# Upper half of the first output panel one copy earlier, and sample numerators of the mLSTM on two column tiles

## The chip, the cores and the metric

The kernel runs on one core of a Trainium2 chip. A core has five engines that run their own instruction streams and meet at semaphores: PE (TensorE, matrix products into PSUM), DVE (VectorE), ACT (ScalarE), POOL (GpSimd) and SP (SyncE, which here only issues DMAs). The metric is the device time of the core in microseconds, from one execution of the whole program; lower is better.

## The reference

Two layers of a decoder trunk run for a prompt of 512 tokens and for 8 sample sequences of 8 tokens each (64 tokens). Each layer is a half-step SwiGLU FFN, a mixer, a second half-step FFN and a gated embedding; layer 0 mixes with latent attention, layer 1 with an mLSTM. All inputs are float32. Cut to what the change touches:

```python
def swiglu(h, w_in, w_out):
    a, b = jnp.split(h @ w_in, 2, axis=-1)
    return (jax.nn.silu(a) * b) @ w_out
...
# one chunk of the mLSTM, per batch b and head h (t, s: tokens; d: 128 keys; v: 256 values)
S = jnp.einsum('bhtd,bhsd->bhts', qc, kc) * jnp.exp(logD - m_t[..., None])
num = jnp.einsum('bhts,bhsv->bhtv', S, vc) + decay[..., None] * jnp.einsum('bhtd,bhdv->bhtv', qc, C)
den = jnp.sum(S, axis=-1) + decay * jnp.einsum('bhtd,bhd->bht', qc, n)
```

For the sample group each of the 8 sequences has its own state C (128 x 256 for a head), so the 64 sample tokens of a head are multiplied by eight different matrices, eight tokens each.

## The kernel before

Activations are kept transposed, channels on partitions and the 576 tokens (512 + 64) on the free axis. A float32 product is made of three products of split operands: a value is an upper part, rounded by a copy to the matmul's format, and a lower part, the rest. For a weight panel in `raw`, ACT writes the upper part `whi` (`upper`, line 1790) and POOL or DVE the lower part `wlo` (`lower`, line 1736, and `panel_lower`, line 2212). A panel is 128 columns of a weight matrix, eight or six chunks of 128 rows.

**The FFNs.** There are four, two in each layer. The 22 hidden blocks of an FFN are cut into three parts of 6, 8 and 8 blocks (`PARTS`), twelve parts in all. In a part PE first makes the hidden blocks one after the other (`pair`, `block_product`, lines 2523 to 2525): seven products of 12 matmuls each, counted by the semaphore `w_done`. Between them ACT copies partial sums from one PSUM bank to another (`copied`, line 1833): the first copy after product 1, the second after product 2, the third after product 3 and the fourth after product 5. PE waits for them by `w_copied`. ACT then applies the SiLU (`gate`), DVE multiplies (`gated`), ACT splits the result (`u_upper`) and DVE its lower part. After the last block of a part PE multiplies the part's hidden values by eight output panels of `w_out` (`out_tile`, which calls `products`, lines 2461 to 2466), one tile of 128 output channels each. A tile may start only when both halves of its panel are there; its chunk n waits for hidden block n.

Every engine runs its instructions in the order in which they stand. The order on ACT is written out in `ffn` (line 1846): a block at a time, with the splitting of the next block's weights between the copies. For the last block of a part (`not more`) there is no next block, and the upper half of the part's first output panel is made instead. It stands behind the fourth copy and ahead of the block's `gate`. It waits for the panel's data (`raw_ready`), for the earlier panels' products and for product 4 of the block before, which is the last to read that slot of `whi`. POOL makes the lower half of the first two panels, DVE of the other six. SP loads the first two panels as soon as their slots of `raw` are free, which is a block before the part's end.

**The mLSTM.** Heads are run one after the other, four in all. For a head PE makes the numerators of the four prompt tiles (`numerators`, line 1563), an output gate panel and the next head's stabilisers, then the sample numerators (`sample_numerators`, lines 1566 to 1576), the states of the samples and of the prompt (`states`, line 1582, `prompt_state`, line 1589) and the next head's scores. `sample_numerators` accumulates nine products of 257 columns in one PSUM bank (256 values and the normaliser), 64 rows high: the within-chunk product, and one for each sequence. The stationary operand of sequence b is a slice of `qdm` that holds the queries of the eight tokens of b in their own columns and zeros in the other 56, so each product writes 64 rows and adds zeros to 56 of them. DVE copies the result to `nu` (line 1404), updates the denominators (lines 1430 to 1439) and then the states `Cb` (line 1409), for which PE waits in turn. ACT makes the next head's decays meanwhile (`decays`, lines 1223 to 1231).

Of the kernel before, what the change touches and what calls it, by code (L numbers as in the profile page):

```python
# [19 lines left out]
TP, TS = 512, 64  # L20
# [3 lines left out]
NB, TB = 8, 8  # L24
# [6 lines left out]
LH, DK, DV = 4, 128, 256  # L31
# [37 lines left out]
def pairs_before(p):  # L69

    n = 0
    for f, name in enumerate(FFNS):
        for q, (a, b) in enumerate(PARTS):
            if p >= P0[name + "_out"] + 8 * q:
                n = NC_F * f + b
    return n
# [62 lines left out]
def hybrid_step(nc, ins, outs):  # L139
    I = ins  # L140
    with ExitStack() as ctx:
        def sem(name):
            return ctx.enter_context(nc.semaphore(name))
# [73 lines left out]
        ps = nc.psum_tensor("ps", [P, 8, 512], F32)  # L217
        ps = ctx.enter_context(ps)
# [28 lines left out]
        w_done, w_copied, w_act = sem("block_products"), sem("sums_copied"), sem("gate_input")  # L247
# [9 lines left out]
        def flat_g(t, i):  # L257

            return t[:, i % 2, :, :].rearrange("p (q c) m -> p q (c m)", q=2)
# [810 lines left out]
        Vt = lu.put("Vt", [P, NTT, LH, DV + 1])  # L1070
        kt = lu.put("kt", [P, NTT, LH, DK])
        Cb = lu.put("Cb", [P, NB, DV + 1])
# [12 lines left out]
        qdm = lu.put("qdm", [P, NB * QDW])  # L1085
# [5 lines left out]
        SD = (SDa, SDb)  # L1091
# [22 lines left out]
        B1, B2, B3, B4, B5 = B0 + 1, 4, 5, 6, 7  # L1114
# [366 lines left out]
        def mlstm_pes(pe, v, products, sums, token_sums, spread, tiles, xgh, xgl):  # L1481
            mm, tr = nc.tensor.matmul, nc.tensor.transpose
# [84 lines left out]
            def sample_numerators(h):  # L1567

                pe.wait_ge(l_SD, NTT * (h + 1))
                pe.wait_ge(l_in, h + 1)  # L1570
                pe.wait_ge(l_nu, 5 * h + 3)
                out = ps[0:TS, B5, 0:DV + 1]
                mm(out, SD[h % 2][0:TS, 1280:1280 + TS], Vt[0:TS, 4, h, :], start=True, stop=False)
                for b in range(NB):
                    ins = mm(out, qdm[:, b * TS:(b + 1) * TS], Cb[:, b, :], start=False, stop=b == NB - 1)
                ins.then_inc(l_num, 1)

            def states(h, b):
# [202 lines left out]
        def _(act):  # L1781
# [8 lines left out]
            def upper(p, dyn, n, place=None, back=1):  # L1790
                hi = place[0] if place else whi[:, p % SPLIT, :, :]
                act.wait_ge(raw_ready[p % RAW], UNIT * (p // RAW - 1 + pairs_before(p) // 2) + dyn * (UNIT // RAW))
                act.wait_ge(panel_used, p - back + dyn)
                act.activation(hi[:, 0:n, :], raw[:, p % RAW, 0:n, :], ACT.Copy).then_inc(whi_ready, 1)  # L1794
# [25 lines left out]
            def third_upper(part, i):  # L1820
                act.wait_ge(g_sum, part.blocks(i, 3))
                act.activation(flat_g(g3h, i), flat_g(g3f, i), ACT.Copy).then_inc(g_hi, 1)  # L1822

            def fourth_upper(part, i):
                g, h = part.g0 + i, 2 * part.half(i) + 1
                act.wait_ge(raw_ready[h], part.loaded(i, h))
                if g:
                    act.wait_ge(w_done, 7 * g)
                act.activation(blocks(g4h), raw_pair(part, i)[:, 3, :], ACT.Copy).then_inc(g_hi, 1)

            def copied(part, i, n, after, dst, src):
                act.wait_ge(w_done, 7 * (part.g0 + i) + after)
                act.activation(dst, src, ACT.Copy).then_inc(w_copied, 1)  # L1833
# [5 lines left out]
            def gate(part, i):  # L1839
                g = part.g0 + i  # L1840
                act.wait_ge(w_act, 2 * g + 2)
                if g:
                    act.wait_ge(w_ub, g)
                act.activation(sA[:, :], tA[:, :], ACT.Silu).then_inc(silu_done, 1)  # L1844

            def ffn(f, last_upper, nxt):
                for part in PART[f]:
                    for i in range(part.n):
                        g, more = part.g0 + i, i + 1 < part.n
                        A, C, B, D_ = [ps[:, part.bank(i) + k, 0:HT] for k in range(4)]  # L1850
                        embed = not part.k and not i
                        if i:
                            fourth_upper(part, i)
                        copied(part, i, 1, 1, B, A)
                        if i == 1 and part.q == 0:
                            gate(part, 0)
                        if i:
                            u_upper(part, i - 1)
                        if g:
                            act.wait_ge(w_act, 2 * g - 1)  # L1860
                        copied(part, i, 2, 2, p5[:, :], D_)
                        if embed:
                            embed_square(0)
                            embed_square(1)
                        if more:
                            first_upper(part, i + 1)
                        copied(part, i, 3, 3, C, B)
                        if embed:
                            embed_square(2)
                            embed_square(3)  # L1870
                        if more:
                            second_upper(part, i + 1)
                        if more:
                            third_upper(part, i + 1)
                        copied(part, i, 4, 5, D_, B)
                        if embed:
                            embed_square(4)
                        if i == 0 and part.q == 0:
                            r_copy(FFNS[f], 1)
                        if not more:  # L1880
                            act.wait_ge(w_done, 7 * (g - 1) + 4)
                            upper(part.p, 0, part.n)
                        if i or part.q:
                            gate(part, i)
                    u_upper(part, part.n - 1)
                    upper(part.p + 1, 0, part.n)
                    if part.q < 2:
                        after = PART[f][part.q + 1]
                        for k in range(2, 8):
                            upper(part.p + k, 0, part.n)  # L1890
                        second_upper(after, 0)
                        third_upper(after, 0)
                        first_upper(after, 0)
                        fourth_upper(after, 0)
                    else:
                        for k in range(8):
                            if k < 6:
                                upper(part.p + 2 + k, 0, part.n)
                            elif k == 6:
                                upper(part.p + 8, 0, last_upper)  # L1900
                            act.wait_ge(tile_taken, part.t + k + 1)
                            x_scaled_upper(nxt, k)
                            x_squares(nxt, k)
# [843 lines left out]
```

## Time and profile before

| | us |
|---|---|
| median of three runs | 2567.34 |
| lowest and highest | 2565.26, 2567.75 |
| the profiled execution, its whole time | 2565.75 |
| its span, first to last instruction | 2563.8 |
| PE busy | 2473.5 (96%) |
| DVE busy | 1684.0 (66%) |
| ACT busy | 1073.0 (42%) |
| POOL busy | 307.7 (12%) |

The granted clock of TensorE is 0.989 of full in the mean. The profiled execution took 1.95 us more than its span and lies 1.59 us under the median. PE is busy in 96% of the span, so most of what other engines do is hidden behind it; what counts is where PE waits, and how long its own instructions take. Line numbers in the profile are those of the kernel before. In the changed kernel lines behind 1575 stand four lower down the file, so a line 1794 of before is 1798 there.

### The profile page before, as it was taken

Reading aid. Unit: us, or ns where it says so; the run is one execution under the profiler, and the core shown is the slowest. Engines: PE = TensorE matmul, PEld = TensorE weight load, DVE = VectorE, ACT = ScalarE, POOL = GpSimd, SP = SyncE. Lnnn points to the kernel's source line nnn. Section 1 sums busy time; section 2 is a strip of 40 time slices with the busy share of each in tenths; the row PEclk is TensorE's granted clock in tenths of the full one; section 3 lists DMA queues with packets and bytes.
Section 4 is the critical chain, followed back from the end, with each engine's and each line's share of the span. In section 5 each row is a group of like instructions: output and inputs, shape, how many; then the busy total and the mean of one; then the engine's idle time right before and its main releaser. Section 6 shows DMA issues by size and latency. Waiting matters only on the chain.

```text
span 2563.8 us, 45161 instructions
## 1 busy us (share of the span) xinstructions
PE 2473.5 (96%) x17653; PEld 2355.3 (92%) x17653; DVE 1684.0 (66%) x2398; ACT 1073.0 (42%) x1780; POOL 307.7 (12%) x247
## 2 busy tenths in 40 slices
PE   6999999999899999999998999999999999999998
PEld 5999999877688999999998999999997789999998
DVE  6676675888555586848568585765434586857666
ACT  6444353455333453525445353443133354443532
POOL 0000001202330100000030000001322200000012
PEclk9999999999899999999999999999999999999999
DMA  4233232222232222333222333332323222332322
GB/s 121 83 99 91 83 94 78 52 49 75 72 110 77 58 79 87 99 87 94 84 78 78 91 91 91 90 91 71 92 69 103 87 66 82 99 99 82 96 76 72
DMA packets 410806, 216.44 MB, mean 84 GB/s; under 512 B 40085, under 2 KB 407834, under 8 KB 410650
## 3 DMA queue, kind: packets, MB, share of 16 engines
q1 hardware_dynamic: 404646, 209.17, 29.0%
q10 hardware_dynamic: 2420, 3.37, 0.4%
q0 software_dynamic: 3584, 1.84, 0.4%
q8 instruction: 95, 1.56, 0.2%
q14 instruction: 61, 0.50, 0.1%
HBM read 206.57 MB, written 7.76 MB: 84 GB/s over the span
## 4 chain that ended last, share of the span: by engine, by line
PE 87%; DVE 7%; ACT 3%; issue 2%; POOL 1%; DMA 0%; SPq 0%; ACTq 0%; DVEq 0%; POOLq 0%
PE ps L2461 13%; PE ps L2463 13%; PE ps L2466 13%; PE ps L2523 12%; PE ps L2524 12%; PE ps L2525 12%; PE ps L1010 2%; DVE st L628 1%; PE ps L924 1%; POOL wlo L1739 1%; PE ps L886 1%; PE ps L875 1%; PE ps L1563 1%; PE ps L972 1%; PE ps L994 1%
## 5 line engine op out<-in xcount | busy, mean ns | idle before, releaser
L1739 POOL TENSOR_TENSOR wlo<-raw,whi 128x1024 fp32r<-128x1024 f32 (+2 forms) x96 | 207.6, 2163 | 1823.0 <-ACT whi L1794 1823.0
L1794 ACT ACTIVATE whi<-raw 128x1024 fp32r<-128x1024 f32 (+2 forms) x175 | 169.4, 968 | 433.1 <-PE ps L2466 432.1
L2461 PE MATMUL ps<-uh,whi 128*128 128x320 f32 (+1 forms) x1408 | 302.2, 296 | 8.0 <-POOL wlo L1739 7.3
L2463 PE MATMUL ps<-ul,whi 128*128 128x320 f32 (+1 forms) x1408 | 301.1, 295 | 0.0
L2466 PE MATMUL ps<-uh,wlo 128*128 128x320 f32 (+1 forms) x1408 | 301.1, 295 | 0.0
L2461 PEld LDWEIGHTS ps<-uh,whi 128*128 128x128 f32 x1408 | 215.9, 188 | 10.7 <-issue 10.5
L2228 DVE TENSOR_TENSOR ub<-ps,r 128x576 f32<-128x576 f32 x96 | 72.7, 757 | 230.7 <-PE ps L2466 215.0
L2466 PEld LDWEIGHTS ps<-uh,wlo 128*128 128x128 f32 x1408 | 216.0, 188 | 0.0
L2463 PEld LDWEIGHTS ps<-ul,whi 128*128 128x128 f32 x1408 | 216.0, 188 | 0.0
L2147 DVE TENSOR_TENSOR wlo<-raw,whi 128x1024 fp32r<-128x1024 f32 x88 | 107.8, 1225 | 130.3 <-ACT whi L1814 130.3
L2461 PE MATMUL ps<-xh,whi 128*128 128x320 f32 x752 | 164.2, 300 | 3.3 <-DVE RB L1280 2.7
L2463 PE MATMUL ps<-xl,whi 128*128 128x320 f32 x752 | 160.6, 295 | 0.0
L2466 PE MATMUL ps<-xh,wlo 128*128 128x320 f32 x752 | 160.4, 295 | 0.0
L1844 ACT ACTIVATE sA<-tA 128x576 f32<-128x576 f32 x88 | 60.4, 686 | 238.5 <-DVE tA L2184 238.5
L1833 ACT ACTIVATE ps<-ps 128x288 f32<-128x288 f32 x264 | 104.3, 395 | 108.3 <-PE ps L2525 107.6
L1822 ACT ACTIVATE g3h<-g3f 128x1024 fp32r<-128x1024 f32 x88 | 93.5, 1062 | 92.1 <-DVE g3f L2141 87.9
L2181 DVE TENSOR_TENSOR ps<-ps,p 128x576 f32<-128x576 f32 x88 | 66.9, 760 | 85.5 <-PE ps L2525 74.0
L2461 PEld LDWEIGHTS ps<-xh,whi 128*128 128x128 f32 x752 | 115.9, 189 | 4.6 <-DVE RB L1280 2.9
L2523 PE MATMUL ps<-xAh,whi 128*128 128x288 f32 x352 | 106.6, 303 | 12.0 <-issue 12.0
L2463 PEld LDWEIGHTS ps<-xl,whi 128*128 128x128 f32 x752 | 115.9, 189 | 0.0
L2466 PEld LDWEIGHTS ps<-xh,wlo 128*128 128x128 f32 x752 | 115.7, 189 | 0.0
L2523 PE MATMUL ps<-xTh,g3h 128*128 128x288 f32 x352 | 104.3, 296 | 5.2 <-DVE xTl L2290 3.7
(425 smaller groups left out, 7085.3 us busy)
## 6 DMA issues: line engine op xcount, KB each, us to landing
raw<-in_w_ffa_in SPq DMA_DIRECT2D x88, 512.0 KB
raw<-in_w_ffb_in SPq DMA_DIRECT2D x88, 512.0 KB
raw<-in_w_ffa_out SPq DMA_DIRECT2D x32, 512.0 KB
pages<-in_cache_ckv SPq DMA_DIRECT2D x128, 128.0 KB, 2.0
raw<-in_w_ffb_out SPq DMA_DIRECT2D x32, 512.0 KB
raw<-in_w_mlstm_in SPq DMA_DIRECT2D x24, 512.0 KB
raw<-in_w_ple_gate SPq DMA_DIRECT2D x16, 512.0 KB
raw<-in_w_ffa_out SPq DMA_DIRECT2D x16, 384.0 KB
```

Of the source, the lines that this page charges most:

```text
L1739: pool.tensor_tensor(lo[:, 0:n, :], raw[:, p % RAW, 0:n, :], hi[:, 0:n, :].bitcast(F32), ALU.subtract).then_inc(wlo_ready, 1)
L1794: act.activation(hi[:, 0:n, :], raw[:, p % RAW, 0:n, :], ACT.Copy).then_inc(whi_ready, 1)
L1822: act.activation(flat_g(g3h, i), flat_g(g3f, i), ACT.Copy).then_inc(g_hi, 1)
L1833: act.activation(dst, src, ACT.Copy).then_inc(w_copied, 1)
L2147: dve.tensor_tensor(wlo[:, s, :, :], raw[:, 2 * part.half(i), :, :], whi[:, s, :, :].bitcast(F32), ALU.subtract).then_inc(g_lo, 1)
L2228: dve.tensor_tensor(ub[:, :], slot(part.t + c, bank), r[:, :], ALU.mult).then_inc(out_read, 1)
L2461: mm(out[:, t], hi[:, n, :], xh_n[:, t], start=first and n == 0, stop=False)
L2463: mm(out[:, t], hi[:, n, :], xl_n[:, t], start=False, stop=False)
L2466: ins = mm(out[:, t], lo[:, n, :], xh_n[:, t], start=False, stop=end)
L2523: mm(out, w_h, m_h, start=fresh and n == 0, stop=False, skip_group_check=not fresh)
L2524: mm(out, w_h, m_l, start=False, stop=False, skip_group_check=not fresh)
L2525: ins = mm(out, w_l, m_h, start=False, stop=n == 3, skip_group_check=not fresh)
```

## The change

Two edits, independent of each other.

1. In ACT's order for the last block of a part, the upper half of the part's first output panel moves from behind the fourth copy to between the third and the fourth, with the wait that belongs to it. That holds for all twelve parts.
2. `sample_numerators` writes its 64 rows as two column tiles of 32. Sequences 0 to 3 own rows 0 to 31, sequences 4 to 7 rows 32 to 63. The within-chunk product is made twice, once for each half, and the eight sequence products take 32 columns of `qdm` in place of 64 and alternate between the halves (0, 4, 1, 5, ...). That makes ten products in place of nine, each with half the rows.

```diff
-                out = ps[0:TS, B5, 0:DV + 1]
-                mm(out, SD[h % 2][0:TS, 1280:1280 + TS], Vt[0:TS, 4, h, :], start=True, stop=False)
-                for b in range(NB):
-                    ins = mm(out, qdm[:, b * TS:(b + 1) * TS], Cb[:, b, :], start=False, stop=b == NB - 1)
+                half = TS // 2
+                for o in (0, half):
+                    mm(ps[o:o + half, B5, 0:DV + 1], SD[h % 2][0:TS, 1280 + o:1280 + o + half], Vt[0:TS, 4, h, :],
+                       start=True, stop=False)
+                for k in range(NB // 2):
+                    for b, o in ((k, 0), (k + NB // 2, half)):
+                        ins = mm(ps[o:o + half, B5, 0:DV + 1], qdm[:, b * TS + o:b * TS + o + half], Cb[:, b, :],
+                                 start=False, stop=k == NB // 2 - 1)
                 ins.then_inc(l_num, 1)
...
                         if more:
                             third_upper(part, i + 1)
+                        if not more:
+                            act.wait_ge(w_done, 7 * (g - 1) + 4)
+                            upper(part.p, 0, part.n)
                         copied(part, i, 4, 5, D_, B)
                         if embed:
                             embed_square(4)
                         if i == 0 and part.q == 0:
                             r_copy(FFNS[f], 1)
-                        if not more:
-                            act.wait_ge(w_done, 7 * (g - 1) + 4)
-                            upper(part.p, 0, part.n)
```

ACT's instructions at the end of the first part (six blocks), before: the fourth block copy is the second of the two that stand in one row, and `whi<-raw` with 128x768 is the output panel.

```order
L1833 ACTIVATE ps<-ps 128x288
L1837 ACTIVATE uh_67<-ub_88 128x576
L1833 ACTIVATE p5_90<-ps 128x288
L1833 ACTIVATE ps<-ps 128x288 x2
L1794 ACTIVATE whi_51<-raw_50 128x768
L1844 ACTIVATE sA_87<-tA_86 128x576
L1837 ACTIVATE uh_67<-ub_88 128x576
```

And in the changed kernel, at the same place:

```order
L1837 ACTIVATE ps<-ps 128x288
L1841 ACTIVATE uh_67<-ub_88 128x576
L1837 ACTIVATE p5_90<-ps 128x288
L1837 ACTIVATE ps<-ps 128x288
L1798 ACTIVATE whi_51<-raw_50 128x768
L1837 ACTIVATE ps<-ps 128x288
L1848 ACTIVATE sA_87<-tA_86 128x576
L1841 ACTIVATE uh_67<-ub_88 128x576
```

One instruction moved past one copy. PE's instructions around the sample numerators of head 0, before:

```order
L1534 MATMUL ps<-RE,cf 128x72
L1573 MATMUL ps<-Vt,SDa 64x257
L1575 MATMUL ps<-Cb,qdm 64x257 x8
L1582 MATMUL ps<-Vt,kwb 128x257 x4
L1589 MATMUL ps<-Vt,kw 128x257 x4
```

And in the changed kernel:

```order
L1534 MATMUL ps<-RE,cf 128x72
L1574 MATMUL ps<-Vt,SDa 32x257 x2
L1578 MATMUL ps<-Cb,qdm 32x257 x8
L1586 MATMUL ps<-Vt,kwb 128x257 x4
L1593 MATMUL ps<-Vt,kw 128x257 x4
```

Nothing moved there; the rows in the result of each product are halved and one product is added.

## Rows read from the trace of the kernel before

**Rows 1.** The page: busy time by engine, and the chain that ended last.

```profile
PE 2473.5 (96%) x17653; PEld 2355.3 (92%) x17653; DVE 1684.0 (66%) x2398; ACT 1073.0 (42%) x1780; POOL 307.7 (12%) x247
...
PE 87%; DVE 7%; ACT 3%; issue 2%; POOL 1%; DMA 0%; SPq 0%; ACTq 0%; DVEq 0%; POOLq 0%
```

**Rows 2.** Groups by form: busy, mean ns of one | idle before, its releasers.

```profile
L2461 PE MATMUL ps<-uh,whi 128*128 128x320 f32 x704 | 218.4, 310 | 8.0 <-POOL wlo L1739 7.3 <-issue 0.7
```

**Rows 3.** Timeline (start, us, what), end of an 8-block part: ACT, POOL, DVE.

```profile
375.38 0.40 ACT L1833 ACTIVATE ps<-ps 128x288 f32<-128x288 f32 x1 [1.12 <-PE ps L2525]
...
378.58 0.40 ACT L1833 ACTIVATE ps<-ps 128x288 f32<-128x288 f32 x1 [2.81 <-PE ps L2525]
378.89 1.05 ACT L1794 ACTIVATE whi<-raw 128x1024 fp32r<-128x1024 f32 x1
...
380.02 2.39 POOL L1739 TENSOR_TENSOR wlo<-raw,whi 128x1024 fp32r<-128x1024 f32 x1 [134.83 <-ACT whi L1794]
...
384.00 0.76 DVE L2173 TENSOR_TENSOR ul<-ub,uh 128x576 fp32r<-128x576 f32 x1 [0.75 <-ACT uh L1837]
...
384.99 2.40 POOL L1739 TENSOR_TENSOR wlo<-raw,whi 128x1024 fp32r<-128x1024 f32 x1 [2.58 <-ACT whi L1794]
```

**Rows 4.** Timeline of PE: an earlier part's last panel (149.27), then this part's end.

```profile
149.27 0.43 PE L2466 MATMUL ps<-uh,wlo 128*128 128x320 f32 x2
149.53 0.30 PE L2523 MATMUL ps<-xAh,whi 128*128 128x288 f32 x1
...
381.45 0.29 PE L2525 MATMUL ps<-xTh,g4l 128*128 128x288 f32 x1
382.67 0.50 PE L2461 MATMUL ps<-uh,whi 128*128 128x320 f32 x2 [0.92 <-POOL wlo L1739]
...
389.13 0.44 PE L2461 MATMUL ps<-uh,whi 128*128 128x320 f32 x2
```

**Rows 5.** Bandwidth in 40 slices from 362 to 376 us (0.35 us each).

```profile
GB/s 0 0 0 51 203 252 329 348 348 347 304 291 288 217 18 0 0 0 0 0 0 0 0 0 0 0 0 0 0 0 0 0 0 0 32 108 197 350 348 347
```

**Rows 6.** Timeline, end of a 6-block part: PE and POOL.

```profile
108.89 1.85 POOL L1739 TENSOR_TENSOR wlo<-raw,whi 128x768 fp32r<-128x768 f32 x1 [57.55 <-ACT whi L1794]
...
110.54 0.29 PE L2525 MATMUL ps<-xTh,g4l 128*128 128x288 f32 x1
...
111.00 0.50 PE L2461 MATMUL ps<-uh,whi 128*128 128x320 f32 x2 [0.16 <-issue]
...
113.87 1.85 POOL L1739 TENSOR_TENSOR wlo<-raw,whi 128x768 fp32r<-128x768 f32 x1 [3.13 <-ACT whi L1794]
...
115.87 0.50 PE L2461 MATMUL ps<-uh,whi 128*128 128x320 f32 x2
```

**Rows 7.** Timeline of PE, sample numerators of head 0.

```profile
1919.29 0.65 PE L1573 MATMUL ps<-Vt,SDa 64*64 64x257 f32 x2
1919.87 3.69 PE L1575 MATMUL ps<-Cb,qdm 128*64 128x257 f32 x16
1923.49 1.56 PE L1582 MATMUL ps<-Vt,kwb 64*128 64x257 f32 x6
```

**Rows 8.** Instructions of line 1575 (all heads): count, ns min/median/max, starts; form.

```profile
L1575 PE MATMUL ps<-Cb,qdm x64: 377/379/432, 1919.9 to 2019.3; 128*64 128x257 f32 x64
```

**Rows 9.** Line 886 from 560 to 570 us: its forms, then its timeline.

```profile
L886 PE MATMUL ps<-PT,Vp x16: 272/433/644, 563.8 to 565.9; 128*64 128x512 f32 x4, 128*64 128x384 f32 x4, 128*64 128x256 f32 x4, 128*64 128x128 f32 x4
...
563.77 2.38 PE L886 MATMUL ps<-PT,Vp 128*64 128x512 f32 x16
```

**Rows 10.** Timeline of ACT and DVE around the sample numerators of head 0.

```profile
1922.32 0.64 ACT L1229 ACTIVATE SDb<-Md,cols 128x128 f32<-128x128 f32 x2
...
1923.60 0.42 DVE L1404 COPY nu<-ps 64x257 f32<-64x257 f32 x1 [3.38 <-PE ps L1575]
...
1925.86 0.16 DVE L1437 TENSOR_TENSOR den<-den 128x5 f32<-128x5 f32 x1
```

**Rows 11.** Stretch from 2002 to 2036 us: busy PE, PEld, DVE, ACT, POOL, then PEclk, DMA.

```profile
2002.00:2036.00 34.00, 29.55 (x163) 23.98 (x162) 15.15 (x44) 8.88 (x18) 9.13 (x6) 0.95 0.38 119
```

## The prediction

> **What bounds the kernel now.** I read the page first: PE is busy in 96% of the span and makes 87% of the chain that ended last [rows 1]. So a gain comes from two places only, a wait of PE that goes or PE work that gets shorter. Then the groups of instructions by form, for what ends PE's idle time ahead of each line: ahead of the products of `uh`, that is of the output tiles, PE waits 7.3 us for POOL's lower half `wlo` [rows 2]. In the timeline this is one wait of 0.92 us at the end of each 8-block part (rows 4 show one; there are eight such parts, and the eight waits read alike), and 8 x 0.92 = 7.36 accounts for the 7.3.
>
> **Edit 1, what it removes.** The chain at the end of an 8-block part: PE ends product 5, ACT makes the fourth copy at 378.58 and then the upper half from 378.89, POOL the lower half from 380.02 to 382.41 [rows 3]; PE starts the tile at 382.67, 0.26 later, while its own last product was issued at 381.45 [rows 4]. ACT stood idle for 2.81 us ahead of the fourth copy [rows 3]. Behind the third copy (375.38) the upper half starts at 375.38 + 0.31 = 375.69 (0.31 is the step from the fourth copy's start to the upper's in the same rows), ends at 376.74, and POOL, 1.13 behind ACT's start as now, runs from 376.82 to 379.21. With 0.26 the tile could start at 379.5, and PE comes for it at 381.58. So the wait goes, with 2.1 us to spare.
>
> What does it do to the fourth copy, which now queues behind the upper? ACT is free at 376.74 and the copy isn't due before 378.58: nothing, with 1.8 us to spare. Does the panel's data stand ready at 375.7? It is the only DMA wait that is moved, and an in-order ACT would hold the fourth copy and so PE. The transfers of the part's first two panels run from about 363 to 367 us [rows 5], so 8 us are to spare. No DMA issue moves. POOL has nothing else there (134.83 us idle ahead of it), so its queue delays nobody.
>
> What is late next? A seam at which nothing waits is the one from a part's last panel to the next part's first block: the pair of matmuls from 149.27 is followed at 149.53 without a gap [rows 4]. So the tile starts 0.13 behind 381.45, at 381.58 in place of 382.67: 1.09 us. After a stall the first weight load also lies open, which makes the first pair 0.50 long in place of 0.43 or 0.44 [rows 4]: another 0.06. That is 1.15 for an 8-block part. The last chunk needs the hidden block's lower half, ready at 384.76 [rows 3], while the tile has 8 chunks in 389.13 - 382.67 = 6.46 us and comes to its last one some 5.5 us after its start, at 387.1. The second tile would start at 381.58 + 6.46 - 0.06 = 387.98; its lower half is ready at 384.99 + 2.40 = 387.39 [rows 3], with 0.26 on top 387.65. That is still ahead, by 0.3 us only, so I keep it as a rival. Later panels are released by PE's progress and move with it. Eight parts: **8 x 1.15 = 9.2 us**. The lower bound is the bare waits, 7.4.
>
> The four 6-block parts are different. There the tile starts at 111.00, 0.26 behind POOL's end at 110.74, and 0.46 behind the last product's start [rows 6]. The page calls it issue, yet it is the same wait, and 0.33 us would go. But the second tile starts at 115.87, while the second panel's lower half is ready only at 113.87 + 1.85 = 115.72 [rows 6]. That one hangs on the last block's `gate` and `u_upper`, which the edit doesn't advance. PE would come for it at 115.5 and wait. I count **0** for these four; the upper bound is 4 x 0.33 = 1.3.
>
> **Edit 2, what it removes.** Each float32 product shows as two records, two passes of PE. The eight sequence products are 16 passes in 3.69 us [rows 7]; with the last one's 0.38 [rows 8] taken off, 15 steps in 3.31, or 0.22 a pass. From line 1573 to line 1582 it is 1923.49 - 1919.29 = 4.20 us for 18 passes [rows 7], 3.96 of it passes and the rest the two changes of shape.
>
> Afterwards there are 20 passes, ten on each tile. What they cost depends on whether the tiles run side by side, and the trace has a case that is nearly this one: line 886, where the two heads of a pair write PSUM partitions 0 to 63 and 64 to 127 in turn, with all 128 rows of the array, float32. Its 16 passes stream 2 x 2 x (512 + 384 + 256 + 128) = 5120 columns [rows 9]. At 0.22/257 = 0.86 ns a column that would be 4.4 us in series and 2.2 for one tile; it takes 2.38, with the end of the last pass in it [rows 9]. So 64-column tiles overlap wholly. I take the same for 32 columns. A tile's line is then 10 passes in place of 18: 8 x 0.22 = 1.76 us less. The two shape changes stay. The nearest bounds: nothing above 1.76 but a shorter open load (0.03 each time), and below it the serial case, which is a loss (rivals).
>
> The Trainium skill, TensorE: Matmul & The Clock Gate (Part 3, Measured speedup), has three column tiles at 2.38 times one after the other, not 3 times. An estimate by that page: two tiles would reach 2 x 2.38/3 = 1.59, so the passes would take 2.8 us and not 2.2, and the whole sum would be about 2 us smaller, near 2553. Line 886 shows no such loss here.
>
> Who follows PE at this place? DVE sits 3.38 us idle until the numerators end, so it had finished its own work at 1923.60 - 3.38 = 1920.2 [rows 10]. The copy to `nu` moves to 1921.84, and denominators, states and the PE waits on them move with it. ACT's decays end at 1922.96 [rows 10], 0.7 us behind the copy's new end (1921.84 + 0.42 = 1922.26), and only then can ACT square `nu`. The square is of the columns that DVE copied in 0.42 us, so it ends near 1923.5, and DVE asks for the result at 1925.86 - 1.76 = 1924.1 [rows 10]: covered by 0.6 us, an estimate. Four heads: **4 x 1.76 = 7.0 us**. In the last head PE waits for DVE ahead of line 1573, but what follows the numerators is the same chain.
>
> **The sum.** 9.2 + 7.0 = 16.2 us. Against the profiled execution: 2565.75 - 16.2 = 2549.55 (span 2563.8 - 16.2 = 2547.6). The median of the runs lies 1.59 above it: 2567.34 - 16.2 = **2551.1 us**, 0.63% less.
>
> **The rivals.**
> - *The tiles overlap with a loss.* If loads came into the open at each pair of passes, each would cost what the first of a row costs: 0.43 against 0.38 [rows 8], 0.05. Ten a head and four heads make 2.0 us: 2553.1. Against it stands line 886, where tiles alternate. 8%. By the Trainium skill's 1.59 (above) the time would be about the same.
> - *The seam of edit 1 closes only in part*, because the second tile waits for its lower half, or leaving the loop costs PE some issue time. Then the gain is 7.4 and not 9.2: 2552.9. For it: the 0.3 us of margin. 12%.
> - *Edit 2 does not do what it says:* tiles of 32 columns are run in turn. Two passes more a head at 0.22 make 4 x 0.44 = 1.8 us more, and only edit 1 is left: 2567.34 - 9.2 + 1.8 = 2559.9. 5%.
> - *Slower: the array empties at each switch of tile.* A pass then takes its whole 0.43 with the load in the open [rows 8] in place of 0.22, and the pause of a change of shape, (4.20 - 3.96)/2 = 0.12 [rows 7]: 0.33 more at each of the eight new switches a head. That is 32 x 0.33 + 1.8 = 12.4 us against 9.2 won, 2570.5. The mechanism decides from (9.2 - 1.8)/32 = 0.23 us a switch. Line 886 speaks against it. 4%. The Trainium skill, TensorEngine Tiling (Array Packing) (Tiling Modes, Key Properties), says that a change of tiling mode drains the engine and a change of tile alone does not; the trace agrees, by line 886.
> - *The clock moves.* Where PE waits, the granted clock sometimes falls from 2.4 to 1.2 GHz for a short stretch: around the last head of the mLSTM it is 0.95 in the mean of 34 us [rows 11], 1.7 us lost. Everything shifts by some us, so one such stretch may come or go: 2549.4 to 2552.8. 5%.
>
> **How the numbers follow.** The forecast has 66%, and its own range is 2548 to 2554. A measurement of this kernel can tell about 0.2%, 5.1 us, from no change. For 8 in 10 the range takes in the first two rivals together (2551.1 + 2.0 + 1.8 = 2554.9) and a clock stretch on either side: 2546.5 to 2557. Faster by over 0.2% (under 2562.2) are the forecast, the first two rivals, the clock, and 3 of the 5% of tiles in turn (the other 2 for a seam that closes badly at the same time): 94%. Within 0.2% lie those 2 and half of the emptying array at the price above: 4%. Slower by over 0.2% is its other half, at a higher price a switch than any row here gives: 2%.
>
> **What would show it.** In the changed profile, PE at the first output tile (line 2465) should have no wait for POOL `wlo` in the 8-block parts, POOL should start 3.2 us ahead of where it did relative to PE's last product, and the fourth copy should still follow PE at once. In the 6-block parts the second tile should start at the same distance from the last product as now. Line 1578 should show 16 passes in about 1.9 us and not 3.69, and DVE's copy to `nu` should come 1.76 us sooner after line 1574's start. The forecast is wrong if line 1578 shows 3.5 us or more, or if a wait of the same size stands at another line behind either place.

## The result, and the profile of the changed kernel

The changed kernel takes 2543.16 us (median of 4 runs, 2539.58 to 2544.42); the kernel before, run beside it, 2566.3 us (4 runs, 2564.12 to 2567.75). The ratio is 0.9908, interval 0.9891 to 0.9925: 23 us less, where the forecast was 16.2 less. The time lies below the range. The profiled execution took 2544.42 us, its span is 2542.6 us against 2563.8 before, a difference of 21.2, with the same mean granted clock, 0.989.

The page of the changed kernel: the line of engines (PE's busy time fell by 16.4 us from [rows 1]), and its group for the output products of `uh`, at line 2465 here.

```profile
PE 2457.1 (97%) x17661; PEld 2342.0 (92%) x17661; DVE 1684.2 (66%) x2398; ACT 1072.7 (42%) x1780; POOL 307.8 (12%) x247
...
L2465 PE MATMUL ps<-uh,whi 128*128 128x320 f32 (+1 forms) x1408 | 296.8, 292 | 1.3 <-POOL wlo L1743 1.3
```

**Edit 1, the seam.** Timeline of the changed kernel at the end of the 8-block part that [rows 3, 4] show: start, duration, engine.

```profile
374.17 2.39 POOL L1743 TENSOR_TENSOR wlo<-raw,whi 128x1024 fp32r<-128x1024 f32 x1 [129.20 <-ACT whi L1798]
375.93 0.40 ACT L1837 ACTIVATE ps<-ps 128x288 f32<-128x288 f32 x1 [1.84 <-PE ps L2529]
...
378.80 0.29 PE L2529 MATMUL ps<-xTh,g4l 128*128 128x288 f32 x1
378.93 0.43 PE L2465 MATMUL ps<-uh,whi 128*128 128x320 f32 x2
```

PE's last block product is followed 0.13 us later by the output tile, the first pair lasts 0.43 and not 0.50, and the 0.92 us of waiting is gone. POOL is done with the panel 2.4 us before PE comes for it. All eight 8-block parts read like this. In the 6-block parts the wait has moved, as the prediction said, from the first tile to the second. Timeline of the first of them:

```profile
116.48 0.50 PE L2465 MATMUL ps<-uh,whi 128*128 128x320 f32 x2 [0.33 <-POOL wlo L1743]
```

**Edit 2, the numerators.** Timeline of PE at head 0, which answers to [rows 7]:

```profile
1905.87 0.62 PE L1574 MATMUL ps<-Vt,SDa 64*32 64x257 f32 x4
1906.43 1.93 PE L1578 MATMUL ps<-Cb,qdm 128*32 128x257 f32 x16
1908.29 1.56 PE L1586 MATMUL ps<-Vt,kwb 64*128 64x257 f32 x6
```

From the first product to the states it is 1908.29 - 1905.87 = 2.42 us, against 4.20: 1.78 less. Heads 1 and 2 read alike, 2.42 against 4.19 and 4.20. The last head does not. Timeline of PE there:

```profile
1996.69 1.03 PE L1574 MATMUL ps<-Vt,SDb 64*32 64x257 f32 x4 [2.16 <-issue]
1997.64 3.16 PE L1578 MATMUL ps<-Cb,qdm 128*32 128x257 f32 x16
2000.74 1.56 PE L1586 MATMUL ps<-Vt,kwb 64*128 64x257 f32 x6
```

It takes 4.05 us against 4.17 before, because the granted clock fell to its lower level (1.2 GHz) behind the wait of 2.16. Stretches of the changed kernel, with the columns of [rows 11] (the granted clock stands ahead of the last two); the third answers to [rows 11]:

```profile
1993.30:1996.70 3.40, 1.24 (x8) 0.79 (x7) 1.95 (x4) 2.16 (x5) 0.21 (x1) 1.00 0.48 144
...
1996.60:2001.00 4.40, 4.31 (x21) 1.66 (x22) 0.14 (x1) 1.49 (x3) 0.00 (x0) 0.61 0.04 12
...
1983.00:2017.00 34.00, 29.54 (x165) 23.41 (x165) 15.33 (x45) 8.88 (x18) 9.13 (x6) 0.90 0.38 122
```

The kernel before has the same wait of 2.16 us and runs the last head at the full clock; its one fall in these 34 us comes later. So the products became shorter four times, 7.1 us of work at the full clock, and 1.65 us of that were lost again to the clock in the last head.

**What was not forecast: the output tiles themselves became faster.** The tiles' matmuls are the same instructions on the same data. Yet the form of 320 columns went from 310 ns in the mean [rows 2] to 303. The groups by form of the changed kernel, whole run:

```profile
L2465 PE MATMUL ps<-uh,whi 128*128 128x320 f32 x704 | 213.4, 303 | 1.3 <-POOL wlo L1743 1.3
```

And a mean of 310 was no duration at all. The kernel before, groups by form in two stretches of 40 us, 390 to 430 us and 1250 to 1290 us, each inside an 8-block part's tiles:

```profile
L2461 PE MATMUL ps<-uh,whi 128*128 128x320 f32 x51 | 15.9, 312 | 0.0
...
L2461 PE MATMUL ps<-uh,whi 128*128 128x320 f32 x52 | 15.7, 303 | 0.0
```

The trace of before holds the same stream at **two paces**, 312 ns and 303 ns. By the starts, a pair of matmuls (320 and 256 columns) steps in 0.267 us at the slow pace and 0.260 us at the quick one; an 8-block tile of 24 pairs takes 6.40 or 6.24 us, a 6-block tile of 18 pairs 4.80 or 4.68. An 8-block part keeps its pace from its first tile to its end, a 6-block part from its second tile on. Four of the eight 8-block parts of before, and all four 6-block parts, were slow; all twelve parts of the changed kernel are quick. In the 6-block part from 972 us of before the first tile was quick and the seven behind it slow. Groups by form, 973 to 976.6 us and 978 to 1008 us:

```profile
L2461 PE MATMUL ps<-uh,whi 128*128 128x320 f32 x5 | 1.5, 303 | 0.0
...
L2461 PE MATMUL ps<-uh,whi 128*128 128x320 f32 x38 | 11.9, 312 | 0.0
```

Between the two stands a second, very short wait: the last pair of the first tile takes 0.37 us to the next start and not 0.26, for the second panel's lower half, which POOL ends at 976.94 and PE takes up at 977.09. So a 6-block part of before is entered out of a wait twice.

What the pace is worth can be read from the starts of two neighbouring parts. Timeline of PE, before, the second part of the first and of the second FFN, with the part behind each ([rows 4] has the one at 382.67):

```profile
240.47 0.50 PE L2461 MATMUL ps<-uh,whi 128*128 128x320 f32 x2 [0.92 <-POOL wlo L1739]
...
1101.69 0.51 PE L2461 MATMUL ps<-uh,whi 128*128 128x320 f32 x2 [0.92 <-POOL wlo L1739]
...
1242.62 0.50 PE L2461 MATMUL ps<-uh,whi 128*128 128x320 f32 x2 [0.92 <-POOL wlo L1739]
```

And the changed kernel at the same places (378.93 is above):

```profile
239.16 0.43 PE L2465 MATMUL ps<-uh,whi 128*128 128x320 f32 x2
...
1095.37 0.43 PE L2465 MATMUL ps<-uh,whi 128*128 128x320 f32 x2
...
1235.14 0.43 PE L2465 MATMUL ps<-uh,whi 128*128 128x320 f32 x2
```

The quick part of before: 1242.62 - 1101.69 = 140.93 us, in the changed kernel 139.77: 1.16 less, which is the seam alone (forecast 1.15). The slow one: 382.67 - 240.47 = 142.20 against 139.77: 2.43 less, of which 1.27 is pace. Added up over the trace: seams 8 x 1.16 = 9.3; numerators 7.1; pace of four 8-block parts 4 x 1.27 = 5.1; pace of four 6-block parts, 4 x 0.83 = 3.3 (from the first start to the last pair's it was 38.42 us and is 37.91, in spite of the 0.33 wait, and the first tile starts about 0.33 sooner behind the last block product). That is 24.8, and the spans differ by 21.2. Of the 3.6 between them 1.7 are the clock around the last head (34 us at 0.90 and not at 0.95) and 0.6 lie ahead of the first part, where the change does nothing. The rest lies where the change does nothing either: 0.7 us between the first FFN and the second, 0.7 behind the last part; why those stretches differ was not traced.

### The profile page after: what moved, and what is told of

The parts are those of the page before. It is cut to its first block, busy times and chain, and to the rows that moved or that the text cites. A ratio compares the mean times of both kernels' runs of the same rounds, so it can differ in the third digit from the quotient of the medians.

```text
span 2542.6 us, 45177 instructions
## 1 busy us (share of the span) xinstructions
PE 2457.1 (97%) x17661; PEld 2342.0 (92%) x17661; DVE 1684.2 (66%) x2398; ACT 1072.7 (42%) x1780; POOL 307.8 (12%) x247
## 3 DMA queue, kind: packets, MB, share of 16 engines
q8 instruction: 95, 1.56, 0.3%
## 4 chain that ended last, share of the span: by engine, by line
PE 87%; DVE 7%; ACT 3%; issue 2%; POOL 0%; DMA 0%; SPq 0%; ACTq 0%; DVEq 0%; POOLq 0%
PE ps L2465 13%; PE ps L2467 13%; PE ps L2470 13%; PE ps L2527 12%; PE ps L2528 12%; PE ps L2529 12%; PE ps L1010 2%; DVE st L628 1%; PE ps L924 1%; PE ps L886 1%; PE ps L875 1%; PE ps L1563 1%; PE ps L972 1%; PE ps L994 1%; PE ps L973 1%
## 5 line engine op out<-in xcount | busy, mean ns | idle before, releaser
L2465 PE MATMUL ps<-uh,whi 128*128 128x320 f32 (+1 forms) x1408 | 296.8, 292 | 1.3 <-POOL wlo L1743 1.3
```

The source lines that it names most:

```text
L2465: mm(out[:, t], hi[:, n, :], xh_n[:, t], start=first and n == 0, stop=False)
```

## The experiments

Lines are compared by the same meter throughout: the mean of the 320-column form (303 ns is all quick, 312 all slow), and the tiles' lengths from their starts.

### Each edit alone

Edit 1 alone (the `sample_numerators` hunk left out), and edit 2 alone (ACT's order as before).

> Edit 1 alone. The forecast's own term is 9.2 us. Theory P (two paces): in the kernel before, the output tiles of eight of the twelve parts run at 0.267 us a pair of matmuls (tile 6.40 us) and in the changed one all at 0.260 (tile 6.24), and this comes from starting the tiles without a wait, so it belongs to edit 1: 9.2 plus about 7 us, 15 to 17 us less than before, and every 8-block part shows tiles of 6.24. Rival N: the faster tiles have to do with edit 2 or with the run; then this kernel is 9 us faster only and shows tiles of 6.40 in some parts.

> Edit 2 alone. Theory P: 4 x 1.78 = 7.1 us less than before, the 0.92 us waits at the 8-block parts stay, and some parts stay at the slow pace (6.40 us a tile). Rival N: 14 us less, with all tiles at 6.24.

Beside a kernel before of 2568.69 us (22 runs), edit 1 alone took 2552.96 us (6 runs), ratio 0.9929 [0.9912, 0.9947], some 16 to 18 us less; edit 2 alone 2560.54 us (11 runs), ratio 0.9963 [0.9949, 0.9977], some 8 to 9.5 less. The page's group for the output products, edit 1 alone and then edit 2 alone (both forms in one row: 292 ns is quick, 297 nearly all slow):

```profile
L2461 PE MATMUL ps<-uh,whi 128*128 128x320 f32 (+1 forms) x1408 | 296.8, 292 | 1.3 <-POOL wlo L1739 1.3
```

```profile
L2465 PE MATMUL ps<-uh,whi 128*128 128x320 f32 (+1 forms) x1408 | 304.1, 297 | 8.0 <-POOL wlo L1743 7.4
```

With edit 1 alone all twelve parts are quick, in tiles of 6.24 and 4.68 us. With edit 2 alone the waits of 0.92 stay and seven of the eight 8-block parts are slow, and all 6-block parts from their second tile on. So the pace comes with edit 1, and the surplus over the forecast is edit 1's: 16 to 18 us where 9.2 were counted. Edit 2 measures as forecast, within its interval.

### The kernel before, traced again, twice

> The kernel before, unchanged, for a second trace. Theory P in the form that the pace is settled by the exact moment at which the wait ends: the set of slow parts may differ from that of the first trace (ffa0 and ffa1, all three parts each, and the 6-block parts of ffb0 and ffb1). If the pace is settled by the program (addresses, places in memory, instruction fetch), exactly the same parts are slow again.

> The kernel before, a third trace, on this chip. Theory (a part entered out of the 0.92 us wait falls at either pace by chance): again some of the eight 8-block parts slow, not the same ones as in the two traces so far, and all four 6-block parts slow at 4.80. Rival (a property of the program, or of a chip): the same four as in one of the two earlier traces.

In the first repeat (2566.21 us) four 8-block parts are slow again, but not the same four: the one near 240 us was slow in the first trace and is quick here, the last one the other way round. Groups by form of the repeat, 245 to 285 us:

```profile
L2461 PE MATMUL ps<-uh,whi 128*128 128x320 f32 x51 | 15.4, 303 | 0.0
```

In the second repeat, on another chip (profiled run 2562.8 us), three are slow, and one of the four 6-block parts is quick, which neither earlier trace had. So the pace is fixed neither by the program nor by the chip: it falls differently in each execution. In these parts it changes only where PE comes out of a wait. The 6-block parts show that best. Five traces, this one among them, have the 6-block parts in the order of before, 20 parts in all; the first tile is slow in 13, the tiles from the second on in 16, and in seven the pace changed at the short wait ahead of the second tile, five times to the slow one and twice to the quick one.

### The wait put back into the changed kernel

```diff
-                    pe.wait_ge(w_ub, part.g0 + part.n - 1)
+                    pe.wait_ge(w_ub, part.g0 + part.n - (part.q != 1))
+                    if part.q == 2:
+                        pe.wait_ge(u_ready, part.g0 + part.n)
```

PE waits at the tiles of the 8-block parts again, but for other work: in the four parts q = 1 for the last block's `ub` (1.56 us), in the four parts q = 2 for both halves of its hidden block (3.12 us).

> The changed kernel with a wait put back ahead of the first output tile: in the second part of each FFN PE waits for the last block's product of gate and value (DVE, about 1.7 us), in the third for its lower half (about 3.2 us), in the first for nothing more. The bare waits cost 4 x 1.7 + 4 x 3.2 = 19.6 us. Theory P: some of the eight parts fall back to 6.40 us a tile, the four without the wait stay fast (4.68), so the loss is above 19.6 by up to 10 us. Rival: the pace has nothing to do with the wait (the earlier POOL work, say); then all stay at 6.24 and the loss is 19.6.

2570.81 us (10 runs), ratio 1.0009 [0.9995, 1.0023] to before. By form, the group of PE:

```profile
L2465 PE MATMUL ps<-uh,whi 128*128 128x320 f32 x704 | 216.9, 308 | 20.0 <-issue 12.5 <-DVE ub L2173 6.2 <-POOL wlo L1743 1.3
```

The 6-block parts, where nothing was put back, are quick. So are all four parts with the 1.56 us wait. Of the four with 3.12 us two are slow (6.40) and two quick (6.24). A wait at the entry thus makes the slow pace possible, not certain; nor does a longer one make it likelier in any way that these numbers show. The span is 27.1 us longer than the changed kernel's. The two waits account for 18.7 and two slow parts for 2.5; another 5.5 is a cost that I had not put into this experiment. Stretches of this trace, with the columns of [rows 11]:

```profile
1720.80:1724.00 3.20, 0.09 (x2) 0.04 (x1) 1.63 (x4) 2.26 (x3) 0.00 (x0) 0.88 0.18 53
1724.00:1733.10 9.10, 9.10 (x49) 9.10 (x50) 0.50 (x1) 0.05 (x1) 2.38 (x1) 0.67 0.20 59
1733.10:1739.00 5.90, 5.90 (x48) 5.90 (x47) 3.38 (x4) 2.42 (x3) 0.00 (x0) 1.00 0.28 85
```

In two of the four 3.12 us waits the granted clock fell to 1.2 GHz while PE stood, and came back some 6 us into the first tile, which took 9.10 us in place of 6.33 in a quick part and 9.16 in place of 6.47 in a slow one: 2.7 to 2.8 us each. In the other two the same wait left the clock at 2.4 GHz.

### The upper moved in the 6-block parts only, and in the 8-block parts only

```diff
-                        if not more:
+                        if not more and part.n == 6:
                             act.wait_ge(w_done, 7 * (g - 1) + 4)
                             upper(part.p, 0, part.n)
                         copied(part, i, 4, 5, D_, B)
```

The other parts keep the upper behind the fourth copy; `part.n == 8` is the second kernel. Both have the numerators of before.

> The kernel before with the upper half moved in the four 6-block parts alone. My prediction counted 0 for them: what the first tile wins the second waits. Theory P: the tiles behind go from 4.80 to 4.68 us, because the second tile's wait is longer and ends at another moment, so 4 x 0.8 = 3.2 us less than before; the 8-block parts keep their waits of 0.92.

> The kernel before with the first panel's upper moved ahead of the fifth copy in the 8-block parts alone: the counterpart of the kernel that moved it in the 6-block parts alone. Theory (pace belongs to the way a part is entered): all eight 8-block parts quick (6.25, then 6.24), the four 6-block parts stay slow (first tile 4.87, second 4.86, then 4.80, 38.4 us in all). Time 12.2 to 12.5 us less than before: 8 x 1.16 = 9.3 of seam and 1.27 for each part that was slow in the kernel before (some 3 on average), so 12 to 13. Rival (the pace is set by the program as a whole, so the 6-block parts follow too): 6-block tiles 4.68. Rival (no pace, seams only): 9.3 less.

6-block parts only: 2560.82 us (11 runs) against 2561.82 for the kernel before on that chip, ratio 0.9996 [0.9986, 1.0005]. The trace shows what was meant: tiles of 5.19, 4.76, then 4.68 us in all four 6-block parts, the 8-block parts with their 0.92 us waits. But of those eight, only one is slow in this trace, with no edit near them. That draw alone is worth 3 x 1.27 us against the first trace, and it can fall as well on the kernel before in other runs. The 3.2 us that I expected do not show in the times: inconclusive by the times, as expected by the trace.

8-block parts only: 2550.69 us (6 runs), ratio 0.9945 [0.9932, 0.9959], 14 us less, with 12 to 13 expected; the interval excludes the 9.3 of the seams alone (0.9964). All eight 8-block parts are quick. The rest went against me: three of the four untouched 6-block parts are quick too. Groups by form, 120 to 145 us and 2156 to 2181 us:

```profile
L2464 PE MATMUL ps<-uh,whi 128*128 128x320 f32 x33 | 10.0, 303 | 0.0
...
L2464 PE MATMUL ps<-uh,whi 128*128 128x320 f32 x31 | 9.7, 312 | 0.0
```

They had been slow in 12 of 12 cases in three traces, and it had looked like a rule; with this kernel and the second repeat it is 16 of 20. The short waits of the 6-block parts leave either pace too. A quick one of these takes 37.60 us, the changed kernel's 37.91: the wait that the edit moves to the second tile is a real one, and the whole gain of the edit in a 6-block part is its pace.

Counted over all traces, an 8-block part that PE enters out of the 0.92 us wait is slow in 19 of 40 cases (4, 4, 3, 7 and 1 of 8); entered without a wait, in none of 48. The tiles behind the 0.33 us wait of the changed 6-block parts are slow in none of 24, so this wait leaves the slow pace rarely, if at all.

That a stream entered without a wait is quick holds for these tiles, not for every stream with the same pair of widths. In layer 0 the 384 matmuls of `oTh` and `oTl`, from some 840 us, follow line 1054 with no idle time ahead of them (their first pair steps in 0.46 us), and they ran at the slow pace in all twelve executions with 320 and 256 columns, the changed kernel's too. Groups by form of the changed kernel, 845 to 890 us:

```profile
L2465 PE MATMUL ps<-oTh,whi 128*128 128x320 f32 x56 | 17.5, 312 | 0.0
```

What fixes the pace there is open.

### The pair of widths

Two kernels with the changed kernel's order and other columns in a pair; the panels and the products are the same.

```diff
-TA = 320
+TA = 288
```

and `TA = 352`, so that a pair is 288 and 288, or 352 and 224 columns.

> The changed kernel with its panels' columns split evenly, 288 and 288, in place of 320 and 256: the products and the columns are the same, only the widths of the two matmuls of a pair differ. Every 288-column step takes 0.133 us in the traces so far, so a pair would take 0.267 us whatever its entry. Theory (there are two paces, and the quick one needs the unequal pair, a 320 that steps off in 140 ns rather than 147): all tiles of 8-block parts 6.40 us and of 6-block parts 4.80 us, even where PE does not wait at the entry, and so 8 x 1.27 + 4 x 0.9 = some 14 us slower than the changed kernel, near 2558. Rival (the quick pace comes from the smooth entry alone): tiles stay at 6.24 and 4.68, and the time stays at the changed kernel's 2543.

> The changed kernel with its panels' columns split 352 and 224, in place of 320 and 256. The sum of the columns is the same. In the traces so far a 288-column step takes 0.133 us, a pair of 320 and 256 takes 0.267 or 0.260 us. Theory (an unequal pair has a quick pace when PE comes to it without waiting): tiles of 8-block parts 6.24 us, as with 320 and 256, or less if the saving grows with the difference (twice the difference, twice the 0.16 us: 6.08 us, some 14 us off the kernel); time 2543, or near 2530. Rival (the quick pace is a property of 320 and 256 alone): 6.40 us, as with 288 and 288, near 2557. Rival (a weight load needs more than the 224-column step gives it): over 6.40, over 2557.

288 and 288: 2558.91 us (10 runs), ratio 0.9985 [0.9971, 0.9999] where the changed kernel has 0.9908 and 0.9923. Every tile of an 8-block part takes 6.40 us, of a 6-block part 4.80 from the third on, although PE enters without a wait. The theory's forecast, near 2558, holds; of the some 14 us that this kernel takes more than the changed one the twelve parts account for 13.3. So the even pair ran at the slow pace in all twelve parts, and the quick one was seen with the uneven pair alone: at every entry of these parts without a wait, and at about half of those out of the 0.92 us wait. 352 and 224: 2592.69 us (4 runs), ratio 1.0089 [1.0065, 1.0114]; tiles of 6.61 and 4.96, a pair in 0.275 us. This is the rival that I had put last. Its span is 49 us longer than the changed kernel's, which ran on another chip. Some 32 of them lie in the twelve parts, the rest in stretches where other products have the same widths; those were not read one by one. By form, the even split and then the wide one:

```profile
L2465 PE MATMUL ps<-uh,whi 128*128 128x288 f32 x1408 | 303.0, 296 | 1.0 <-POOL wlo L1743 1.0
```

```profile
L2465 PE MATMUL ps<-uh,whi 128*128 128x352 f32 x704 | 233.6, 332 | 0.3
L2465 PE MATMUL ps<-uh,whi 128*128 128x224 f32 x704 | 186.4, 265 | 0.0
```

That the weight load is what the 224-column step cannot hold is argued, not shown: the loads read 187 to 193 ns in all these kernels.

### The order of the two column tiles

```diff
-                for k in range(NB // 2):
-                    for b, o in ((k, 0), (k + NB // 2, half)):
+                for o in (0, half):
+                    for k in range(NB // 2):
+                        b = k + (NB // 2 if o else 0)
```

> The changed kernel with the sequence products in another order: first the four of rows 0 to 31, then the four of rows 32 to 63. Theory O (PE hands products on in their order, and two overlap only if neighbours go to different tiles): the 16 passes take about 3.5 us and not 1.9, 4 x 1.6 = 6.4 us more than the changed kernel. Rival (the queue looks far enough ahead to run the other tile's products early): no difference.

2543.45 us (4 runs), ratio 0.9924 [0.9905, 0.9944]. Timeline of head 0:

```profile
1904.22 2.83 PE L1579 MATMUL ps<-Cb,qdm 128*32 128x257 f32 x16
1906.97 1.56 PE L1587 MATMUL ps<-Vt,kwb 64*128 64x257 f32 x6
```

2.83 us, not 1.93 and not the 3.5 of passes strictly one after the other. By the traces the alternation is worth 0.9 us a head, 3.6 in all. The times can't show that: the changed kernel had 2544.45 us on the same chip, and the two intervals, each some 4 to 5 us to either side, lie over each other. Nor can the spans of the two profiled executions, because of the stretch of 34 us around the last head. Here PE's clock was at 0.95 in it and in the changed kernel's profiled execution on that chip (the second row) at 0.80, which is 34 x 0.15 = 5.1 us, an estimate:

```profile
1983.00:2017.00 34.00, 29.55 (x171) 24.17 (x171) 15.80 (x47) 8.88 (x18) 9.16 (x6) 0.95 0.40 126
```

```profile
1985.00:2019.00 34.00, 29.72 (x144) 22.71 (x143) 15.18 (x44) 8.89 (x18) 8.02 (x6) 0.80 0.40 127
```

PE still saves 0.86 us against before (3.69), so some passes of the two tiles overlap in this order too. The starts of the 16 passes show which: four stand alone, 0.22 us apart, then come four pairs whose two passes start 6 to 29 ns apart, then four alone again. That is 12 steps of some 0.22 us, where the alternating order has 8; so the second half of the first tile's passes runs beside the first half of the second tile's. A pass of 32 columns that stands alone steps in the same 0.22 us as one of 64 did, so the gain is the overlap and not the narrower pass.

### The changed kernel again, and a second panel ahead

```diff
+                        if not more:
+                            act.wait_ge(w_done, 7 * g + 4)
+                            upper(part.p + 1, 0, part.n)
                         if i == 0 and part.q == 0:
...
                     u_upper(part, part.n - 1)
-                    upper(part.p + 1, 0, part.n)
```

It stands right behind the fourth copy, ahead of the last block's gate, and makes the lower half of the second panel early, for which the second tile of a 6-block part waits.

> The changed kernel again, for comparison on the same chip and for a second trace: 21 to 23 us less than before. Theory P: all twelve parts run at the fast pace again (6.24 and 4.68 us a tile), since no wait stands ahead of their first tile.

> The changed kernel, with the upper half of the second output panel moved as well, from behind the last block's gate and upper copy to right behind the fourth copy. In the changed kernel the 6-block parts still wait 0.33 us for that panel's lower half (their first tile takes 5.19 us, the second 4.76, later ones 4.68). Theory P: the wait goes and all tiles run at 4.68 to 4.7, so 4 x 0.5 = 2 us less than the changed kernel; the 8-block parts gain nothing. Rival: ACT's gate comes later behind the extra copy and PE waits there; then no gain or a loss.

On one chip, beside a kernel before of 2561.82 us: the changed kernel 2544.45 us (6 runs), ratio 0.9923 [0.9908, 0.9938], all twelve parts quick again; with the second panel ahead 2536.89 us (4 runs), ratio 0.9896 [0.9879, 0.9914], the shortest of all. Its group by form, and its timeline in the first part:

```profile
L2467 PE MATMUL ps<-uh,whi 128*128 128x320 f32 x704 | 213.1, 303 | 0.0
```

```profile
109.08 1.85 POOL L1743 TENSOR_TENSOR wlo<-raw,whi 128x768 fp32r<-128x768 f32 x1 [1.36 <-ACT whi L1798]
```

POOL has the second panel at 110.93, where the changed kernel had it at 116.34; PE waits nowhere at these products, and a 6-block part takes 37.33 us and not 37.91. That is 4 x 0.58 = 2.3 us. The medians lie 7.6 apart and the spans 7.4 (2546.8 and 2539.4). The other 5.1 of the spans are the clock around the last head, 0.95 in this execution and 0.80 in the changed kernel's. Whether the earlier panel has a part in that was not tested, and what makes up the other 5 us between the medians is open; the gain that its own place shows is 2.3 us.

## Why the prediction was wrong in size and right in mechanism

- *The seam of an 8-block part*, forecast 1.15: measured 1.16. Its parts (wait 0.92, gap to 0.13, first pair 0.50 to 0.43) each show. Neither the fourth copy nor the second tile became late: the 0.3 us of margin at the second tile held, in all eight.
- *The 6-block parts, forecast 0 by seams*: right as to the waits: 0.33 won at the first tile and a wait of 0.33 at the second. Wrong in the sum, by 0.83 a part.
- *The numerators*, forecast 1.76 a head: measured 1.78, 1.77 and 1.78, and 0.12 in the last head, where the clock took the rest. Line 1578 takes 1.93 us. The two tiles of 32 columns overlap wholly, and the time of 10 passes holds 20. The loss that the prediction took as an estimate from the Trainium skill's 2.38 for three tiles (TensorE: Matmul & The Clock Gate, Part 3, Measured speedup) does not show.
- *The step that failed* is the one behind "What is late next?": the tile's length of 6.46 us [rows 4] was taken from one part and used as a constant, and the sum of an entry's cost ended where the wait ended. An entry out of a wait also left the stream behind it at the slow pace, for 50 us in half the 8-block parts and for some 34 us in all four 6-block parts. The missing term is 5.1 us in the 8-block parts and 3.3 in the 6-block ones, 8.4 in all; 16.2 + 8.4 = 24.6, less 1.7 for the clock below, is 22.9, against 23.1 by the medians and 21.2 by the spans. That it comes so near the medians is partly luck, since runs of one kernel differ by some 4 us and more. That the term belongs to edit 1 is shown by each edit alone; that it is the wait and not the order of ACT, by the wait put back.
- *It could have been seen.* The mean of 310 ns in [rows 2] was a mixture of 312 and 303; the 8-block parts in that trace differ by 142.20 to 140.93. The prediction looked at one part of eight and let it stand for the others, on the ground that their waits read alike. Their waits did, their tiles did not.
- *The rivals*: one of them came true beside the forecast. "The clock moves" named the stretch around the last head at 0.95 and 1.7 us; with the numerators on two tiles that stretch had 0.90 and 0.80 (the changed kernel, twice), 0.85 (edit 2 alone), 0.90 (the wait put back) and 0.95 (the second panel ahead, the two other widths and the tiles in turn). With the numerators of before it had 0.95 in five of six executions (the kernel before three times, edit 1 alone, the 6-block parts only) and 0.90 in the sixth (the 8-block parts only). So it lay under 0.95 in four of eight against one of six; that the narrower products make a fall there likelier is not shown. The seam, the loss between tiles and the emptying array did not come. The range failed at its lower end, because apart from one stretch of clock it held only costs that could spoil the gain; nothing else in it could make the gain larger.

What stays open is the mechanism by which a wait, or its end, sets the pace. It was not found which moment of the entry gives which pace. In the twelve parts an entry without a wait gave the quick one every time; the products of `oTh`, with no idle time ahead of them and always slow, show that this is not the whole rule.

## What to carry to other kernels

Before taking a duration as a constant, read it in several copies of the same stage: a mean between two values that each occur is a sign of two states, and what sets the state can be worth as much as the wait that is being removed. Where a long stream of matmuls is entered out of a wait, price the stream behind it as well as the wait, with its quick pace as the upper bound of the gain. And where a draw of that kind is in the kernel before, one of its traces is not enough to tell what an edit elsewhere did.

## What the runs showed of the hardware that was not expected

- Back-to-back pairs of 320 and 256 columns (fp32r, a weight load for each) ran at 0.260 or at 0.267 us a pair, at the same granted clock of 2.4 GHz, for stretches of 33 to 51 us. In the twelve parts pairs of 288 and 288 took 0.267, pairs of 352 and 224 0.275, in one execution each.
- Two column tiles of 32, float32 with 128 rows, overlap wholly when they alternate: 16 passes in 1.93 us. Four products of one and then four of the other take 2.83: the last four passes of the first run beside the first four of the second.
- A wait of 3.12 us inside a busy stretch brought the granted clock to 1.2 GHz in two of four cases, and the first tile behind it took 9.1 us in place of 6.3. The wait of 2.16 us ahead of the last head was followed by such a fall in five of eight executions with the numerators on two tiles (the last head took 4.05, 3.55, 3.14, 3.89 and 4.10 us in place of 2.42), and in none of six with the numerators of before, whose last head took 4.17 us each time. At the entries of 0.92 and 1.56 us no trace shows one.
